# Two layers of a hybrid decoder trunk on one core: conv products dealt out between attention steps, units in head pairs, the position term as a column, output weights in two halves

## What is computed

```
h    = rms_norm(x, norm1);  proj = h @ w_in
q, kc, vc, ks, vs, kw, vw, gates, cb, cc, ch = split(proj)
kc, vc = compress(kc + pos), compress(vc + pos)   # windows of 32 tokens, stride 16 -> 31 rows
         # flat @ w1 (2048 -> 128), gelu, @ w2 (128 -> 64)
o_attn = g0 * attn(q, kc, vc) + g1 * attn(q, ks, vs) + g2 * attn(q, kw, vw)   # 8 heads, 2 kv heads,
         # causal, plus a bias by distance; with 512 tokens all blocks are selected
o_conv = cb * conv3(cc * ch)                       # 512 channels, three taps along the tokens
x += concat(rms_norm(o_attn), rms_norm(o_conv)) @ w_out
x += swiglu(rms_norm(x))  in layer 0;  top-2-of-8 experts of the same kind in layer 1
```

## Time and profile before

| | |
|---|---|
| median of 3 runs | 2555.46 us |
| lowest and highest of them | 2554.8, 2587.93 us |
| the profiled execution | 2586.12 us, its span 2584.3 us |
| TensorE busy | 2450.6 us, 95% of the span |
| VectorE, ScalarE, POOL busy | 406.8, 282.6, 70.3 us |
| mean granted clock of TensorE | 0.895 |
| data moved | 382.85 MB, 148 GB/s over the span |

### The profile page before, as it was taken

How to read it: one execution, slowest core, us unless ns; L and a number is a source line. 1 busy time by engine, 2 the same in 40 slices (tenths; PEclk the granted TensorE clock), 3 DMA queues, 4 the chain that set the end, 5 groups by cost and what they waited for, 6 DMA issues and landing times.

```text
span 2584.3 us, 29996 instructions
## 1 busy us (share of the span) xinstructions
PE 2450.6 (95%) x12924; PEld 1804.8 (70%) x12924; DVE 406.8 (16%) x1078; ACT 282.6 (11%) x752; POOL 70.3 (3%) x79
## 2 busy tenths in 40 slices
PE   7998999899999998998999679999999999999995
PEld 3565666444444444565664579999999999999994
DVE  1112332200000002113342300000101010110102
ACT  1102222100000001102231000000000000000000
POOL 1100000000000001100000000000000000000001
PEclk9887556999999998987589689999999999999997
DMA  6012000252221041001000286577777777878753
GB/s 243 33 65 81 1 1 8 91 201 71 76 81 65 0 180 41 33 1 65 1 1 1 96 322 224 218 270 264 278 278 278 277 280 292 294 293 307 290 217 106
DMA packets 43700, 382.85 MB, mean 148 GB/s; under 512 B 5330, under 2 KB 5362, under 8 KB 14512
## 3 DMA queue, kind: packets, MB, share of 16 engines
q1 hardware_dynamic: 35920, 355.68, 36.7%
q0 software_dynamic: 4768, 14.92, 1.8%
q10 hardware_dynamic: 2880, 10.32, 1.0%
HBM read 368.46 MB, written 14.54 MB: 148 GB/s over the span
## 4 chain that ended last, share of the span: by engine, by line
PE 93%; DVE 3%; DMA 1%; issue 1%; ACT 1%; POOL 0%; POOLq 0%; DVEq 0%; ACTq 0%
PE ps L353 26%; PE ps L362 13%; PE ps L965 12%; PE ps L763 8%; PE ps L974 6%; PE ps L863 5%; PE ps L757 5%; PE ps L883 5%; PE ps L950 4%; PE ps L874 2%; PE ps L832 1%; PE ps L829 1%; DVE work L1018 1%; PE ps L334 1%; PE ps L310 1%
## 5 line engine op out<-in xcount | busy, mean ns | idle before, releaser
L353 PE MATMUL ps<-work,arena 128*128 128x136 f32 (+3 forms) x5632 | 703.9, 283 | 0.7 <-issue 0.7
L353 PEld LDWEIGHTS ps<-work,arena 128*128 128x128 f32 x5632 | 685.9, 191 | 1.2 <-issue 0.8
L362 PE MATMUL ps<-hid,arena 128*128 128x136 f32 (+3 forms) x2816 | 364.7, 283 | 0.0
L362 PEld LDWEIGHTS ps<-hid,arena 128*128 128x128 f32 x2816 | 348.4, 191 | 0.1
L965 PE MATMUL ps<-hT,arena 128*128 128x512 f32 x704 | 305.2, 597 | 0.8 <-issue 0.8
L965 PEld LDWEIGHTS ps<-hT,arena 128*128 128x128 f32 x704 | 134.8, 192 | 170.8 <-issue 170.8
L763 PE MATMUL ps<-hT,arena 128*128 128x512 f32 x448 | 203.4, 615 | 0.0
L523 DVE TENSOR_TENSOR hid<-sg,ps 128x136 f32<-128x136 f32 (+3 forms) x176 | 52.7, 299 | 899.3 <-ACT sg L624 898.7
L883 PEld LDWEIGHTS ps<-arena,work 128*128 128x128 f32 x640 | 121.5, 273 | 95.2 <-issue 89.2
L763 PEld LDWEIGHTS ps<-hT,arena 128*128 128x128 f32 x448 | 87.9, 198 | 109.2 <-issue 109.0
L863 PE MATMUL ps<-arena 64*128 64x128 f32 (+3 forms) x256 | 159.3, 722 | 0.0
(11 more groups left out here) (200 smaller groups left out, 1075.3 us busy)
## 6 DMA issues: line engine op xcount, KB each, us to landing
arena<-m_w SPq DMA_DIRECT2D x176, 1536.0 KB, 6.5
arena<-f_gu SPq DMA_DIRECT2D x22, 1024.0 KB, 6.0
arena<-w_cv SPq DMA_DIRECT2D x8, 1536.0 KB, 22.7
arena<-f_dn SPq DMA_DIRECT2D x11, 1024.0 KB, 4.8
arena<-w_o SPq DMA_DIRECT2D x2, 4096.0 KB, 12.2
arena<-w_q SPq DMA_DIRECT2D x2, 2048.0 KB, 12.6
arena<-w_kv SPq DMA_DIRECT2D x2, 2048.0 KB, 17.2
arena<-bias_by_query_and_key SPq DMA_DIRECT2D x2, 2048.0 KB, 8.9
```

The source lines that it names most:

```text
L353: m = mm(ps[:, s % 2, j * CAP:j * CAP + W], w[:, k, :], xT[:, k, 0:W], start=(k == 0), stop=(k == KD - 1))
L362: m = mm(ps[:, 2 + j // 2, (j % 2) * CAP:(j % 2) * CAP + W], down_w[s % NSLOT][:, j * P:(j + 1) * P], hid[:, s % 2, 0:W], start=(s == 0 an ...
```

## The change

What it does:

- The conv group's twelve thirds (a third is B, C or h of a chunk, 8 products) go through one PSUM bank, 3, in the order C, h, B and with chunks in the order 2, 3, 0, 1. The first third stands before the compression product, the second behind it, and the other 80 products are dealt out over 30 of attention's steps by the table `STEP_FILL`. Each third waits until the last one's reader on ScalarE or VectorE is through. The element-wise work is split into parts that stand in the attention loops of VectorE and ScalarE.
- Attention's steps are 32 (and two to run out). A step p handles two units, two heads of one branch; the branch alternates from step to step. All turns go through bank 2.
- The position vectors stand as 16 more columns behind each of the two windows' tokens in `Z`, so that the compression product has 66 columns in place of 62 and needs no product of its own for the position term.
- Output weights come in two loads of 2 MB, one after the compression product, one after six conv thirds; the next stage's second weight tile may also be loaded before the output product.
- The bias table's products stand first on TensorE, before the first norm; POOL issues the constants, the table and the one-hot matrix ahead of the gain, and makes the bias table's DRAM copies before it serves the q norms.
- The last tile's turn and the conv norm's four sums stand beside the output product.

```diff
+STEP_FILL = ((1, 1, 1), (1, 1, 1), (1, 1, 0)) + 2 * ((0, 1, 1), (1, 1, 1), (1, 1, 1)) + (
+    (0, 1, 3), (1, 1, 1), (0, 1, 0), (0, 1, 1), ...
...
-        WO = arena[:, A_WO:A_WO + KD * D].rearrange("p (k n) -> p k n", k=KD)
+        WO = [arena[:, a:a + 4 * D].rearrange("p (k n) -> p k n", k=4) for a in (A_WO, A_WC)]
...
-                sp.wait_ge(pcv_done, CT * (L + 1))
-                sp.dma_start(WO, w_o[L]).then_inc(wo_in, 16)
+                sp.wait_ge(hp_done, L + 1)
+                sp.dma_start(WO[0], w_o[L, :, 0:4, :]).then_inc(wo_in[0], 16)
+                sp.wait_ge(pcv_done, 3 * CT * L + 6)
+                sp.dma_start(WO[1], w_o[L, :, 4:KD, :]).then_inc(wo_in[1], 16)
...
+            pe.wait_ge(table_in, 32)
+            pe.wait_ge(zeroed, 1)
+            for i in range(2):
+                m = mm(ps[0:H, i, 0:320], table_sb[0:33, :], oh_sb[0:33, i * 320:(i + 1) * 320], start=True, stop=True)
+            m.then_inc(bias_ps, 1)
...
+                def fill(n):
+                    for _ in range(n):
+                        third, k = divmod(given[0], KD)
+                        i, j = third // 3, (1, 2, 0)[third % 3]
+                        if k == 0:
+                            if third == 0:
+                                pe.wait_ge(qt_done, TT * L + 4)
+                            elif j == 2:
+                                pe.wait_ge(cc_done, CT * L + i + 1)
+                            elif j == 0:
+                                pe.wait_ge(zc_done, CT * L + i + 1)
+                            else:
+                                pe.wait_ge(cv_done, CT * L + i)
+                            if j == 1:
+                                pe.wait_ge(wcv_in[CO[i]], 16 * (L + 1))
+                        m = mm(ps[:, 3, :], cv_w[CO[i]][:, k, j * P:(j + 1) * P], hT[:, k, :], start=(k == 0), stop=(k == KD - 1))
...
-                        mm(ps[:, 3, a * P:a * P + 2 * NCMP].rearrange("p (g n) -> p g n", g=G), W1[:, a, l, :],
-                           Z[:, a, :, l:l + 8 * NCMP - 7:8], start=(l == 0), stop=(l == LP - 1))
-                    for l in range(LP):
-                        m = mm(ps[:, 3, a * P + 100:a * P + 101], W1[:, a, l, :],
-                               pc[:, PC_POS + a * LP + l:PC_POS + a * LP + l + 1], start=(l == 0), stop=(l == LP - 1))
+                        m = mm(ps[:, 5, a * P:a * P + 66].rearrange("p (g n) -> p g n", g=G), W1[:, a, l, :],
+                               Z[:, a, :, l:l + ZC - LP + 1:8], start=(l == 0), stop=(l == LP - 1))
...
-                    if u >= 2:
-                        pe.wait_ge(pta if u % 2 else ptd, 32 * L + u // 2)
+                    elif u % 2:
+                        pe.wait_ge(ptd, NP * L + (u + 1) // 2)
+                    else:
+                        pe.wait_ge(pta, NP * L + u // 2)
                     for i in range(t + 1):
-                        m = tr(ps[:, 2 + u % 2, i * P:(i + 1) * P], sb_p[:, u % 2, i * P:(i + 1) * P], ident)
+                        m = tr(ps[:, 2, i * P:(i + 1) * P], sb_p[:, u % 2, i * P:(i + 1) * P], ident)
...
-                for i in range(64 + 3):
-                    t, r = i // 16, i % 16
-                    if 2 <= i < 66:
-                        turn(i - 2)
-                    if i < 64:
-                        scores(i)
-                    if i >= 3:
-                        values(i - 3)
+                for p in range(NP + 2):
+                    t, q = p // 8, p % 8
+                    f = STEP_FILL[p] if p < len(STEP_FILL) else (0, 0, 0)
+                    if p < NP:
+                        scores(2 * p)
+                        scores(2 * p + 1)
+                    fill(f[0])
+                    if 1 <= p <= NP:
+                        turn(2 * p - 2)
+                    fill(f[1])
+                    if p >= 2:
+                        values(2 * p - 3)
+                    if 1 <= p <= NP:
+                        turn(2 * p - 1)
+                    fill(f[2])
+                    if 1 <= p <= NP:
+                        values(2 * p - 2)
...
                     if t == 1:
+                        o_turn(TT - 1)
+                        pe.wait_ge(rc_done, L + 1)
                         pe.wait_ge(ot_done, TT * (L + 1))
```

More of the change, by code:

```diff
@@ L44, with third_ends @@
 ZLEN = 640
+ZC = S // 2 + LP
+CO = (2, 3, 0, 1)
+NP = TT * H
+NU = 2 * NP
+STEP_FILL = ((1, 1, 1), (1, 1, 1), (1, 1, 0)) + 2 * ((0, 1, 1), (1, 1, 1), (1, 1, 1)) + (
[3 rows of a table added]
+assert sum(sum(f) for f in STEP_FILL) == 10 * KD and len(STEP_FILL) <= NP
+def third_ends():
+    ends, n = {}, 2 * KD
+    for p, f in enumerate(STEP_FILL):
+        for _ in range(sum(f)):
+            n += 1
+            if n % KD == 0:
+                ends[p] = n // KD - 1
+    return ends
+THIRD_END = third_ends()
+assert sorted(THIRD_END.values()) == list(range(2, 3 * CT))
 SLOT = 3 * KD * P
@@ L62 @@
 A_W1 = A_KV
-A_WO = CT * SLOT - KD * D
-assert A_END <= ARENA and A_WO >= SLOT
+A_WO = A_KV
+A_WC = 2 * SLOT
+assert A_END <= ARENA and 2 * LP * HID <= KD * 512 and CO[2:] == (0, 1) and KCW * KD >= 2 * S
 C_ID, C_ONE, C_TRI, C_IOTA = 0, P, 2 * P, 3 * P
@@ L185, in build @@
         wcv_in = [sem(f"wcv_in{c}") for c in range(CT)]
-        w1_in, wo_in, T_in = sem("w1_in"), sem("wo_in"), sem("T_in")
+        w1_in, T_in = sem("w1_in"), sem("T_in")
+        wo_in = [sem(f"wo_in{i}") for i in range(2)]
         slot_in = [sem(f"slot_in{s}") for s in range(NSLOT)]
@@ L711, in _ @@
                 sp.dma_start(kc_w, w_kc[L]).then_inc(wkc_in, 16)
-                for c in range(CT):
+                for c in CO:
                     sp.dma_start(cv_w[c], w_cv[L, c]).then_inc(wcv_in[c], 16)
@@ L811, in layer @@
[L811 to L823 removed]
+                given = [0]
@@ L834, in layer @@
                 m.then_inc(hp_done, 1)
-                conv(2)
+                fill(KD)
                 pe.wait_ge(gelu_done, L + 1)
@@ L938, in layer @@
                 for t in range(TT):
+                    m = mm(ps[:, 6, t:t + 1], sqsum[:, t * P:(t + 1) * P], ones[:, 0:1], start=True, stop=True)
+                m.then_inc(cs_ps, 1)
+                for t in range(TT):
+                    if t == 0:
+                        pe.wait_ge(wo_in[0], 16 * (L + 1))
+                        pe.wait_ge(wo_in[1], 16 * (L + 1))
+                        pe.wait_ge(cvm_done, CT * (L + 1))
+                        pe.wait_ge(sb_done, NU * (L + 1))
+                        pe.wait_ge(ptd, NP * (L + 1))
+                        pe.wait_ge(pta, NP * (L + 1))
@@ L1007, in _ @@
             dve.wait_ge(const_in, 16)
+            dve.wait_ge(bias_ps, 1)
+            for i in range(2):
+                m = v.tensor_copy(bias_row[:, 320 * i:320 * (i + 1)], ps[0:H, i, 0:320])
+            m.then_inc(bias_sb, 1)
             def norm(ns):
```

340 lines of the change are left out of this document (181 added, 159 removed), and 3 rows, old and new, of the table STEP_FILL.

## The result

| | before | changed |
|---|---|---|
| time, median | 2569.9 us (4 runs, 2554.8 to 2587.93) | 2333.16 us (4 runs, 2329.48 to 2333.99) |
| ratio | | 0.9073 [0.8995, 0.9152] |
| profiled execution | 2586.12 us, span 2584.3 | 2332.5 us, span 2330.7 |
| mean granted clock | 0.895 | 0.966 |

From profiled execution to profiled execution the gain is 253.6 us where the sum said 184.2: 69.4 us more than forecast. The rest of this text is mostly about those 69.4.

The account below looks back on a forecast made before the run. The prediction took attention to be bound by TensorE at its lower clock level. Savings of -201.1 us and costs of +16.9 took the profiled 2586.12 us to 2402 us; range 2378 to 2462, chance 80%.

Parts of the forecast that it names:

- Pairs of heads, one bank for the turns: Attention steps: second turn's wait for the first's copy, about 3.9 us, hides under TensorE's 6.8 us step; no cost.
- Clock, -146.0: Attention in both layers: wide conv products between steps keep the upper clock level throughout, -90.4 and -55.6 us.
- Position term and the block's second half: Compression block: one-column instructions vanish, -23.9 us; the shorter block's second half takes 5 instead of 6.93, -3.8 us.
- Weight loads, +7.4: Dealt-out conv products: 74 groups per layer each expose 0.05 us of weight load, +7.4 us, from a range 0 to +17.
- One bank for the thirds: Conv thirds: ten handovers per layer wait for the bank's reader, 0.2 us each, +4 us, from a range 0 to +18.
- VectorE's first steps: Early attention: VectorE does conv work and compressed keys ahead of the third and fourth scores, +4 us, up to +10.
- Last turn, -10.5: Before the output product: waits of 5.27 and 5.26 us hide under 32 wide instructions, -10.5 us.
- Bias table: Its products move to the kernel's start, removing waits of 2.29 and 0.77 us at 109 us: -3.1 us.
- Tail of conv, -13.8: Ahead of attention: the 5.98 us wait goes and norm sums move to the upper clock level, -13.8 us for both layers.
- the first three: Attention: clock stays at 0.50 (2752 us, 4%), rises late (2462 us, 6%), or copies bound steps (2466 to 2530 us, 7%).
- the third: Attention steps become bound by copies, adding 1 to 2 us to each of 64 steps: 2466 to 2530 us, chance 7%.
- The fourth: Attention: clock swings, from the single bank, with half the stretch at the lower level: +175, 2577 us, chance 3%.

Follow-up runs that it names:

- run 2: Changed kernel with the second head's scores moved behind the first turn of the step, no longer beside the first head's: 2381.5 us, 48.3 more than the changed kernel.
- run 5: Kernel before, with one added wide product ahead of every unit's scores but the first two (62 a layer): 2560.38 us, ratio 1.0035 to before.
- run 3: Kernel before, with 8 unused wide products per layer filling TensorE's 5.98 us idle gap ahead of attention: 2541.83 us, ratio 0.9918 to before.
- run 8: Changed kernel with the position term's 64 one-column instructions per layer put back, result unused: 2366.99 us, 33.8 more than the changed kernel.
- run 9: Changed kernel with the last tile's turn ahead of the output product again, as before: 2342.84 us, 9.7 more than the changed kernel.
- run 7: Changed kernel with the same 80 conv products in ten bunches of 8, one every third step: 2410.75 us, 77.6 more than the changed kernel.
- run 1: Changed kernel with each pair's heads chosen from the same 64 partitions, order of work unchanged: 2354.75 us, 21.6 more than the changed kernel.
- run 11: Changed kernel with one conv product moved from step 28 to 30 and one moved within step 26: 2328.17 us, 5.0 less than the changed kernel.
- run 4: Kernel before, with one added wide product ahead of every second unit's scores (32 a layer): 2556.01 us, ratio 1.0002 to before.

## Why the prediction was wrong

It had the sign, the main mechanism and most terms, and it was wrong in size: it forecast 7.1% of the profiled execution, and 9.8% came.

- **The step that failed** is "Pairs of heads, one bank for the turns", costed as "Hidden". It asked only whether the copies hide under "TensorE's own step", and took that step as "2 x 2.53 + 2 x 0.87": two heads cost twice one head. They do not. Two neighbouring score products in different row halves take the time of one (1.06 us for four instructions where two took 1.06), and the changes between 64-row and 128-row work are halved. Apart again, they cost 48.3 us (run 2). Had the step been bounded from both sides as the others were, its lower end would have been the whole second score product. The rows said 64 rows and not 128, and I read the columns only.
- **Clock, -146.0**: right in kind and about in size. The clock is 1.00 in attention from the first steps, and run 5 shows that wide products alone bring and hold the level, for some 133 us of the same kind. But the reason given, that the attention mix "keeps whichever level it has", is too simple for the small tiles: with the level at 1.00 on entry they lost it behind a wait of 1.78 us (run 3), and with wide products at half the density it swings (run 4). The four 256-column products that the prediction saw ahead of each rise stand in every tile; in the first tile of the kernel before, at 248 us, no rise followed them. Narrow products alone lost the level without any wait (run 8); whether attention's mix would, or whether its waits cost the level, stays open.
- **Position term and the block's second half, -23.9 and -3.8**: mis-sized by some 6; 33.8 measured (run 8). Missing was the rise of the clock behind the block, 3.1 us a layer in run 8 (in the kernel before, the 48 wide instructions there took 22.57 and 23.68 us instead of 20.81), and the block's second half takes 3.9 us, not 5.
- **Weight loads, +7.4**: not seen. A wide product between others takes 0.86 to 0.87, one behind scores 0.96, as any product there does. So no run shows the 0.05 us a group. It was not tried alone.
- **One bank for the thirds +4, VectorE's first steps +4**: about right in sum. The changed kernel's waits are 4.6 us in layer 0 and much the same in layer 1, but about 3 of each come at the turns, and the two short falls of the clock cost some 3 us more.
- **Last turn, -10.5**: 9.7 (run 9). **Bias table**, -3.1: -3.2 (q's start to conv's took 84.86 instead of 88.09 us). **Start**, +1.5: +0.9 (q starts at 24.24 instead of 23.32), with the transposes at 14.89. **Tail of conv, -13.8**: its wait is gone; not tried by itself. **Output weights**: 0, no wait for them.

The trace of before had a sign of the failed step as well, in the compressed branch's scores, whose heads alternate between the halves:

```profile
399.21 1.92 PE L895 MATMUL ps<-kcT,arena 64*128 64x31 f32 x16
```

That is 0.12 us an instruction at the lower level, where one-column instructions of 128 rows took 6.73 / 32 = 0.21.

Put together: 46.9 for the paired scores, 12.8 for the changes of row count, 7.4 not paid for loads, 6.1 for the block make 73, and the falls of the clock take some 3 back: 70, where 69.4 were missing. The first two are prices of rows times counts, which for run 2 came out 6 us too high, so that the closeness of the sum is partly luck.

Of the rivals, the first three did not come, the third only in run 7. The fourth did in miniature. After TensorE had waited 1.0 us for the conv bank at 157 us the clock stood at 0.58 from 158 to 161 us, and after the wait of 1.7 us at 0.56 for 3 us; in layer 1 the same waits left it at 1.00. The rule of the Trainium skill ("TensorE: Matmul & The Clock Gate", section on psum-queue depth-cycling), that short idles between groups that cycle through PSUM make the clock swing, describes this. The trace agrees in kind, with these two falls, and not in size: a swing of half the time did not follow from one bank, and the +29 that the prediction set beside its sum did not come.

For the failed step the Trainium skill has the rule that was not used ("TensorE: Matmul & The Clock Gate", Part 3 on packing small matmuls): products in different row groups of the array run at once. The trace agrees, at 1.06 us for both against 1.91 in the same group (run 1). The Trainium skill's "TensorEngine Tiling (Array Packing)", section Key Properties, adds that a change of the tiling mode drains TensorE; the 0.1 us on each side of the scores fits that, though no run shows that it is a drain.

## What to carry to other kernels

Where a product contracts over 64 partitions or fewer, put its neighbour in the other half of the partitions right beside it, and keep such products together; when you cost a reordering, read the row counts of neighbours and not only the columns. Independent wide products are worth more dealt evenly among small ones than in a block or in bunches (run 7): they hold the clock and cover the small steps' handovers, and how many are needed has to be tried (one per two units swung, one per unit held). End the dealing one or two steps ahead of what reads its result, early enough for the last element-wise work and late enough to cover the last copies.

## What the runs showed of the hardware

- Two float32 products of 64 rows, in different halves, neighbours: 1.06 us together at 512 columns and 0.42 at 128; in one half 1.91 and 0.64; apart 1.05 and 0.42 each. Their place in the partitions and in the order decided this; each wrote its own bank, and one bank for both was not tried.
- Products beside them are 0.1 us longer on either side: wide 0.96 for 0.87, values 0.94 for 0.84, turn 0.54 for 0.44.
- TensorE, entered into small products at the upper level, fell to 1.2 GHz 1.3 us behind a wait of 1.78 us and stayed there for 116 us of almost unbroken work (run 3). With one wide product per two units it rose at 252 us, fell at 272 behind waits of 0.91 and 1.61 us and rose again at 300 (run 4); with one per unit it rose at 236 us and held through waits of 0.91 and 0.76 us (run 5).
- A wait of 1.0 or 1.7 us in dense small work can be followed by about 3 us at the lower level (layer 0 of the changed kernel), or by none (layer 1, the same waits); in run 11 the 1.0 us wait was followed by a fall in both layers.
